# Second input projection of a two-layer kernel: six column blocks by one level of Strassen's algorithm, in two passes of half the tokens

## The chip, the cores and the metric

One Trainium2 chip, one core. The metric is the device time of one execution in microseconds (us). The kernel runs as a single launch.

## The reference

Two blocks over a sequence of 2048 tokens with width 1024, in float32. The first is RMS norm, a pooling mixer and a residual. The second takes its output, normalises and modulates it, and does

```python
proj = h @ w_in + b_in                      # (2048, 1024) @ (1024, 4624)
na_q, na_k, na_v, na_z, ml_q, ml_k, ml_v, ml_o, ml_z, i_f, f_f, i_b, f_b = split(proj)   # nine blocks of 512, four gates of 4
na_out = neighbourhood_attention(na_q, na_k, na_v, rpb) * silu(na_z)
qk = silu(centred_short_conv(concatenate([ml_q, ml_k]), conv_w, conv_b))                 # 5 taps over the tokens
hm = (mlstm forward + mlstm backward) * sigmoid(ml_o)
ml_out = normalised(hm) * ml_norm_w * silu(ml_z)
y = concatenate([na_out, ml_out]) @ w_out
```

with a gated residual and a final RMS norm. The change is in `h @ w_in` and in what stands directly around it.

## The kernel before, in words

Each engine runs one instruction stream in order; semaphores tie them together, and the order within each stream is written out by hand. SyncE (SP) and GpSimd (POOL) issue the DMAs, a few come from ScalarE (ACT).

**Precision.** Every large operand is held as two float32r parts, high (a ScalarE copy) and low (a VectorE subtraction). `mm3` (lines 143 to 147) multiplies high x high, high x low and low x high: three matmuls for each 128x128 by 128x512 piece.

**Stages.** `Mixer` and `FirstOut` make the first block, whose output goes to DRAM transposed as hT2. While `FirstOut` runs, `GatedWeights` multiplies `w_out` by the gate, splits it and stores it. `Proj` is the second input projection, `States` the mLSTM gates and states, `Attention` the neighbourhood attention, `Tail` the rest.

**Proj before.** All of h stays in SBUF as split halves (`iT`, 4 token blocks of 512). Nine blocks of 512 weight columns follow one another: nq, nk, mv, mk, mq, nv, nz, mz, mo. Six are column blocks: a unit is 128 weight columns, stationary, with 512 tokens moving, one item (24 matmuls) for each unit and token block. mv, nv and mo are row blocks: an item is 128 tokens, stationary, by 512 columns, again 24 matmuls. Each weight unit is loaded once (512 KB, line 1389) and split once (lines 1438 and 1443). After an item its PSUM bank is read: ScalarE adds the bias or takes SiLU (lines 1544, 1562, 1567), VectorE makes the low part of nq and nk (line 1633), the five taps of the convolution for mk and mq (line 1618) or the bias sum of the row blocks (line 1653), ScalarE takes the sigmoid of mo (line 1578), and GpSimd issues the stores (mk and mq at line 1672, mo at line 1697).

**States.** `States` is called after each item on every engine, one tick an item, from the fourth nv item on (first the gates, then 31 steps). A step loads keys (lines 2312, 2318) and values into the one buffer `sv` (line 2322, on SyncE, after the previous step's weighing), weighs them on GpSimd into the one buffer `swv` (line 2378), multiplies (line 2397), updates the state on VectorE (line 2358) and stores it (line 2327). TensorE's step at an item uses the weighing that GpSimd did one tick earlier.

**The end of Proj before.** 16 mo items. At mo item 3 SyncE issues attention's first 16 loads of 256 KB (`hd`, line 1835), at 7 its z and v loads, at 11 its tables (line 1852). Attention's first scores stand before the last mo item's matmuls (`first_pe`).

## Time and profile before

| | |
|---|---|
| Time, median of 3 runs | 1884.34 us (1883.26 to 1884.55) |
| Profiled execution: span | 1883.3 us |
| Profiled execution: own time | taken as its span, no other figure is shown |
| TensorE busy | 1865.6 us, 99% |
| VectorE, ScalarE, GpSimd busy | 982.4, 618.3, 552.5 us (52, 33, 29%) |
| Granted TensorE clock, mean | 0.999 of 2.4 GHz |
| DMA | 303.55 MB, mean 161 GB/s |

Rows of matmuls give the duration of one from its start to its end; they overlap, so their distance is shorter. Waits that a row attributes to a releaser are inferred from semaphore events. Windows give, for each stretch, its length and each engine's busy time with the number of instructions, the granted clock as a share of 2.4 GHz, the DMA engines' busy share and GB/s.

### The profile page before, as it was taken

Reading aid. Unit: us, or ns where it says so; the run is one execution under the profiler, and the core shown is the slowest. Engines: PE = TensorE matmul, PEld = TensorE weight load, DVE = VectorE, ACT = ScalarE, POOL = GpSimd, SP = SyncE. Lnnn points to the kernel's source line nnn. Section 1 sums busy time; section 2 is a strip of 40 time slices with the busy share of each in tenths; the row PEclk is TensorE's granted clock in tenths of the full one; section 3 lists DMA queues with packets and bytes.
Section 4 is the critical chain, followed back from the end, with each engine's and each line's share of the span. In section 5 each row is a group of like instructions: output and inputs, shape, how many; then the busy total and the mean of one; then the engine's idle time right before and its main releaser. Section 6 shows DMA issues by size and latency. Waiting matters only on the chain.

```text
span 1883.3 us, 26698 instructions
## 1 busy us (share of the span) xinstructions
PE 1865.6 (99%) x10035; PEld 1540.4 (82%) x10035; DVE 982.4 (52%) x2117; ACT 618.3 (33%) x1317; POOL 552.5 (29%) x925
## 2 busy tenths in 40 slices
PE   9999999999999999999999999999999999999998
PEld 8888878888888888888888787888887777788886
DVE  6556565775666433114777322223213777776665
ACT  7321111233444432101222202221114667655552
POOL 2112222233642222110110000222314777544442
PEclk9999999999999999999999999999999999999999
DMA  6223142366897745312221123665563776867663
GB/s 197 95 79 119 62 128 81 104 184 235 306 266 252 235 168 162 101 50 84 74 78 68 53 62 116 211 211 171 168 220 105 243 232 224 271 219 241 230 229 112
DMA packets 236365, 303.55 MB, mean 161 GB/s; under 512 B 41414, under 2 KB 161126, under 8 KB 236204
## 3 DMA queue, kind: packets, MB, share of 16 engines
q1 hardware_dynamic: 205724, 215.84, 37.4%
q0 software_dynamic: 23600, 77.61, 11.4%
q10 hardware_dynamic: 6912, 8.39, 1.2%
q8 instruction: 80, 1.31, 0.3%
q14 instruction: 49, 0.40, 0.1%
HBM read 194.71 MB, written 107.54 MB: 160 GB/s over the span
## 4 chain that ended last, share of the span: by engine, by line
PE 94%; DVE 2%; DMA 2%; issue 1%; ACT 1%; POOL 0%; SPq 0%; POOLq 0%; DVEq 0%; ACTq 0%
PE banks L145 25%; PE banks L147 25%; PE banks L146 25%; PE banks L2106 3%; PE banks L2069 3%; PE banks L2088 3%; PE banks L2704 2%; PE banks L2706 1%; PE banks L2397 1%; DMA iraw<-in_w_in 1%; PE banks L2089 1%; PE banks L2674 1%; PE banks L234 1%; PE banks L1109 1%; PE banks L1741 0%
## 5 line engine op out<-in xcount | busy, mean ns | idle before, releaser
L145 PE MATMUL banks<-hT,wu 128*128 128x512 f32 (+1 forms) x528 | 204.6, 387 | 1.1 <-DVE wu L512 0.6
L147 PE MATMUL banks<-hT,wu 128*128 128x512 f32 (+1 forms) x528 | 202.3, 383 | 0.0
L146 PE MATMUL banks<-hT,wu 128*128 128x512 f32 (+1 forms) x528 | 202.2, 383 | 0.0
L145 PE MATMUL banks<-iT,wub 128*128 128x512 f32 x384 | 151.2, 394 | 0.0
L145 PE MATMUL banks<-iT,wua 128*128 128x512 f32 x384 | 150.8, 393 | 0.0
L145 PE MATMUL banks<-wub,iT 128*128 128x512 f32 x384 | 150.6, 392 | 0.0
L147 PE MATMUL banks<-iT,wub 128*128 128x512 f32 x384 | 149.7, 390 | 0.0
L147 PE MATMUL banks<-iT,wua 128*128 128x512 f32 x384 | 149.5, 389 | 0.0
L146 PE MATMUL banks<-wub,iT 128*128 128x512 f32 x384 | 149.5, 389 | 0.0
L147 PE MATMUL banks<-wub,iT 128*128 128x512 f32 x384 | 149.5, 389 | 0.0
L146 PE MATMUL banks<-iT,wua 128*128 128x512 f32 x384 | 149.5, 389 | 0.0
L146 PE MATMUL banks<-iT,wub 128*128 128x512 f32 x384 | 149.4, 389 | 0.0
L1653 DVE TENSOR_TENSOR st<-banks,br 128x512 f32<-128x512 f32 x48 | 33.1, 692 | 201.0 <-PE banks L147 193.5
L145 PEld LDWEIGHTS banks<-hT,wu 128*128 128x128 f32 x528 | 99.3, 188 | 25.3 <-ACT ub L470 4.3
L147 PEld LDWEIGHTS banks<-hT,wu 128*128 128x128 f32 x528 | 99.2, 188 | 19.6
L146 PEld LDWEIGHTS banks<-hT,wu 128*128 128x128 f32 x528 | 99.3, 188 | 18.5
L1932 ACT ACTIVATE p<-s,ast 128x480 f32<-128x480 f32 (+1 forms) x128 | 83.7, 655 | 53.0 <-DVE ast L1970 53.0
L145 PE MATMUL banks<-ws,ys 128*128 128x512 f32 x256 | 100.5, 393 | 0.0
L147 PE MATMUL banks<-ws,ys 128*128 128x512 f32 x256 | 99.8, 390 | 0.0
L146 PE MATMUL banks<-ws,ys 128*128 128x512 f32 x256 | 99.7, 389 | 0.0
L1618 DVE SCALAR_TENSOR_TENSOR ca<-cu,cw,ca 128x512 f32<-128x512 f32 (+2 forms) x128 | 96.3, 752 | 4.5
L2039 POOL TENSOR_SCALAR p<-p,ast 128x384 f32<-128x384 f32 (+1 forms) x128 | 71.9, 562 | 46.2 <-DVE ast L1976 44.8
(293 smaller groups left out, 4116.3 us busy)
## 6 DMA issues: line engine op xcount, KB each, us to landing
iraw<-in_w_in SPq DMA_DIRECT2D x36, 512.0 KB, 4.4
wa<-in_w_ada SPq DMA_DIRECT2D x48, 256.0 KB
...
xr<-in_x SPq DMA_DIRECT2D x16, 512.0 KB, 4.4
h<-h POOLq DMA_DIRECT2D x16, 512.0 KB, 4.3
hT<-tr POOLq DMA_DIRECT2D x16, 512.0 KB, 5.1
tws<-wg SPq DMA_DIRECT2D x16, 512.0 KB, 5.1
```

The lines of the kernel that those rows point to most:

```text
L145: e.matmul(ps, lh, rh, start=first, stop=False)
L146: e.matmul(ps, lh, rl, start=False, stop=False)
L147: return e.matmul(ps, ll, rh, start=False, stop=last)
L234: t = e.transpose(self.tp[m][g][:, j * P:(j + 1) * P], self.x[m][:, (4 * g + j) * P:(4 * g + j + 1) * P], self.ident[:])
L1618: e.scalar_tensor_tensor(out=a[:, left:right], in0=cur[:, left + x:right + x], scalar=cw[:, x, ch:ch + 1], in1=a[:, left:right], op0=ALU.m ...
L1653: e.tensor_tensor(self.st[i % 2][:], pb, self.br[:, x % 2, :], ALU.add).then_inc(*self.row_step.inc())
L1932: e.activation(self.pr[n % 8][:, 0:N], self.sr[n % 4][:, 0:N], ACT.Exp, bias=self.st[:, n, 0:1], scale=-1.0, accum_out=self.st[:, n, 1:2]) ...
L2039: e.tensor_scalar(rows[:, :, 0:P], rows[:, :, 0:P], self.st[:, n, 2:3], 1.0, ALU.mult, ALU.mult).then_inc(*self.scaled.inc())
L2069: t = e.matmul(self.pS[(2 * p + hh) % 4][:, 0:N], b[r, q, (2 * i + a) * P:(2 * i + a + 1) * P], keys, start=x == 0, stop=x == 2)
L2088: e.transpose(self.pT[x][:, j * P:(j + 1) * P], probs[:, 160 * j:160 * j + P], self.ident[:])
L2106: t = e.matmul(self.pO[d, 0:P], v, self.ptr[(2 * q + hh) % 4][r, j * P:(j + 1) * P], start=(j == 0), stop=(j == nb))
L2704: t = e.matmul(o, self.eb[c % 2][d][:, h, :], self.v1[c % 2][:, h, :], start=True, stop=not self.inter(c, d))
```

## The change

The six column blocks are grouped in pairs of units (a quad: two units of 128 columns by two token blocks of 512, the 1024 of the sum cut in two). A quad takes seven products of 12 matmuls instead of eight (Strassen's algorithm in Winograd's form). The tokens are done in two passes of 1024: in each, mv, gates, nv (and in the first pass mo) as row items for 8 token tiles, then 12 quads, and after the second pass's quads the last 8 mo items.

Per quad, GpSimd forms four sums of weights (S1 to S4) before they are split; per pass it forms four sums of tokens (T1 to T4), 1024 wide, in two rounds. Seven weight operands a quad are split on ScalarE and VectorE, 512 wide, into a ring of nine slots. Products 1, 6, 7, 4 follow one another in one PSUM bank and 5, 3 in another without a new start, so the sums of products arise in PSUM; ScalarE copies the partial sums out after 5, 1 and 6, and TensorE goes on in that bank when the copy is made. VectorE joins copy, bank and bias (`join`), and for a convolution quad does four taps on each of two token blocks (the first tap is now ScalarE's); GpSimd stores.

States' ticks lie beside the second pass's quads (every second or third product) and then two to an item in the first seven mo items, on TensorE one in the middle and one at the end of an item. The state has two buffers now; `sv` and `swv` still one each. Attention's first 16 loads are issued at mo item 0, the tables at 1, z and v at 4. ml_norm_w is multiplied into the gated weights and no longer into mz.

The diff, cut to its core:

```diff
-def mm3(e, ps, lh, ll, rh, rl, first, last):
-
-    e.matmul(ps, lh, rh, start=first, stop=False)
-    e.matmul(ps, lh, rl, start=False, stop=False)
-    return e.matmul(ps, ll, rh, start=False, stop=last)
+def mm3(e, ps, lh, ll, rh, rl, first, last, more=False):
+    e.matmul(ps, lh, rh, start=first, stop=False, skip_group_check=more)
+    e.matmul(ps, lh, rl, start=False, stop=False, skip_group_check=more)
+    return e.matmul(ps, ll, rh, start=False, stop=last, skip_group_check=more)
...
+            if j // 2 < 4:
+                e.tensor_tensor(self.lo[j % 2][:], self.raw[j % 2][:], self.hi[j % 2][:].bitcast(F32), ALU.subtract).then_inc(*self.low.inc())
+            else:
+                w.wait_ge(*proj.col_in.ge(5))
+                e.scalar_tensor_tensor(out=self.lo[j % 2][:], in0=self.raw[j % 2][:], scalar=proj.mw[:, j // 2 - 4:j // 2 - 3],
+                                       in1=self.hi[j % 2][:].bitcast(F32), op0=ALU.mult, op1=ALU.subtract).then_inc(*self.low.inc())
...
+QUADS = ((("mk", "nz"),) * 4 + (("mq", "mz"),) * 4 + (("nk", "nq"),) * 4,
+         (("mk", "nz"),) * 4 + (("nk", "nq"),) * 4 + (("mq", "mz"),) * 4)
+COLUMN = {"nq": 0, "nk": 1, "nv": 2, "nz": 3, "mq": 4, "mk": 5, "mv": 6, "mo": 7, "mz": 8}
 ROW_BLOCKS = ("mv", "nv", "mo")
+NQ = 12
+PRODUCTS = 7 * NQ
...
+        work = [("mv", m) for m in range(8)] + [("gates", 0), ("gates", 1)] + [("nv", m) for m in range(8)] + [("mo", m) for m in range(8)]
...
+        work += self.products(0)
...
+        work += [("mv", m) for m in range(8, NT)] + [("gates", 2), ("gates", 3)] + [("nv", m) for m in range(8, NT)]
...
+        work += self.products(1)
+        self.mo0 = len(work)
+        work += [("mo", m) for m in range(8, NT)]
+        self.work = work
...
+                q = x[2]
+                self.place.append({"5": self.y[q % 2], "3": self.y[q % 2], "2": self.z}.get(x[0], self.x[q % 2]))
...
+        out = [("5", ps, 0)]
+        for q in range(NQ):
+            out += [(x, ps, q) for x in "12637"] + ([("5", ps, q + 1)] if q < NQ - 1 else []) + [("4", ps, q)]
+        return out
...
+        at = {11: [("t", 0, 0)], 13: [("t", 0, 1)], self.second + 9: [("t", 1, 0)], self.second + 11: [("t", 1, 1)]}
+        for ps in range(2):
+            c0 = self.c0[ps]
+            for q in range(NQ):
+                for steps, n in ((("S1", "S3"), 7 * q - 9), (("S2",), 7 * q - 6), (("S4",), 7 * q - 4)):
+                    if q == 0 and steps[0] == "S1":
+                        n = -2
+                    at.setdefault(c0 + max(n, -2 if q == 0 and steps[0] == "S1" else -1), []).extend(("s", ps, q, x) for x in steps)
+            at[c0 - 1].sort(key=lambda x: (x[2], ("S2", "S4", "S1", "S3").index(x[3])))
...
+        c0 = self.c0[1]
+        at = [c0 + 2 * i for i in range(18)] + [c0 + 36 + 2 * i for i in range(11)] + [c0 + 59 + 3 * i for i in range(9)]
+        self.ticks = {n: [i] for i, n in enumerate(at)}
+        t = len(at)
+        for m in range(7):
+            self.ticks[self.mo0 + m] = [t + 2 * m, t + 2 * m + 1]
+        self.ticks_sp = {}
+        order = sorted(self.ticks)
+        for a, b in zip(order, order[1:]):
+            self.ticks_sp.setdefault(a + 1 if a + 1 < b else b, []).extend(self.ticks[b])
...
+        if j[0] == "a":
+            w.wait_ge(*self.full.ge(self.product_of(j) + 1))
+        elif j[2] == 7:
+            w.wait_ge(*self.full.ge(self.last_item(j[1]) + 1))
+        else:
+            w.wait_ge(*self.kdone.ge(7 * j[1] + j[2] + 1))
...
+        s = (q + 1) % 2
+        r = self.raw[s].rearrange("p a (k c) -> p (a k) c", k=4)
+        if q < 2:
+            w.wait_ge(*self.done(("row", 2 + 2 * ps, 3 + 4 * q)))
+        else:
+            w.wait_ge(*self.done(("a", ps, q - 2, ("S4", "S3", "A22")[part])))
+        name, j = self.unit(ps, q, part > 0)
+        c = COLUMN[name] * W + j * P
+        ks = (slice(0, KT), slice(0, 4), slice(4, KT))[part]
+        dst = (slice(0, KT), slice(KT, KT + 4), slice(KT + 4, 2 * KT))[part]
+        e.dma_start(r[:, dst], self.win[:, ks, c:c + P]).then_inc(*self.raw_in[s].inc())
...
     def sp(self, e, att, states):
...
+            if n >= mo0:
+                att.early_sp(e, w, n - mo0)
+            for t in self.ticks_sp.get(n, ()):
+                states.sp(e, w, t)
...
+    def act_task(self, e, w, ps, q, t):
+        g, cu, ca, key = self.g, self.cu, self.ca, (ps, q)
+        conv = self.kind(ps, q) == "conv"
+        if t in (1, 3):
+            x, b = ("1", 0) if t == 1 else ("6", 1)
+            w.wait_ge(*self.full.ge(self.item[(x, ps, q)] + 1))
+            self.copy_wait(w, ps, q, x)
+            if not conv:
+                self.free(w, ("g0", "g1")[b], (ps, q, b))
+            else:
+                for y in [y for y in self.nkq if y < (ps, q)][-1:]:
+                    self.stored(w, y + (b,))
+                if (ps, q) == (0, 0):
+                    for i in range(2):
+                        w.wait_ge(*self.out.t_st[i].ge(8))
+            e.activation(g[b][:], self.bank(ps, q, x), ACT.Copy).then_inc(*self.copied.inc())
+        if conv:
+            i = self.convs[key]
+            ch = (4 if QUADS[ps][q][0] == "mk" else 0) + q % 4
...
+                w.wait_ge(*self.joined.ge(3 * NQ * ps + 3 * q + 1 + x))
+                w.wait_ge(*self.conv_u.ge(3 * i + (1, 3)[x]))
+                self.free(w, ("ca0", "ca1")[x], (ps, q, x))
+                e.activation(ca[x][:, left:right], cu[x][:, left:right], ACT.Identity, bias=self.cb[:, ch:ch + 1],
+                             scale=self.cw[:, 0, ch:ch + 1]).then_inc(*self.tapped.inc())
+            if t == 6:
+                w.wait_ge(*self.joined.ge(3 * NQ * ps + 3 * q + 3))
+                e.activation(g[5][:], g[5][:], ACT.Silu).then_inc(*self.evac.inc())
...
+            if t in (6, 9):
+                x = t // 9
+                left, right = self.edge(ps, x)
+                w.wait_ge(*self.conv_step.ge(8 * i + 4 * x + 4))
+                e.activation(ca[x][:, left:right], ca[x][:, left:right], ACT.Silu).then_inc(*self.evac.inc())
+        else:
+            if t in (3, 5):
+                x = t // 5
+                w.wait_ge(*self.joined.ge(3 * NQ * ps + 3 * q + 1 + x))
...
+            if name == "5":
                 w.wait_ge(*self.full.ge(n + 1))
+                self.copy_wait(w, x[1], x[2], "5")
+                e.activation(self.g[2][:], self.pg(n), ACT.Copy).then_inc(*self.copied.inc())
+            for ps, q, t in self.tasks(n):
+                self.act_task(e, w, ps, q, t)
...
+    def join(self, e, w, ps, q, t):
+        g, cu = self.g, self.cu
+        conv = self.kind(ps, q) == "conv"
+        c = 3 * NQ * ps + 3 * q
+        if t not in (2, 4, 5):
+            return
+        x = {2: "2", 4: "3", 5: "7"}[t]
+        w.wait_ge(*self.full.ge(self.item[(x, ps, q)] + 1))
+        w.wait_ge(*self.copied.ge(c + {2: 2, 4: 3, 5: 1}[t]))
+        pb, b = self.bank(ps, q, x), self.bias(ps, q, int(t == 5))
...
+    def dve_task(self, e, w, ps, q, t):
+        g, cu, ca = self.g, self.cu, self.ca
+        c = 3 * NQ * ps + 3 * q
+        if self.kind(ps, q) == "conv":
+            i = self.convs[(ps, q)]
+            ch = (4 if QUADS[ps][q][0] == "mk" else 0) + q % 4
+            x = int(t > 5)
+            left, right = self.edge(ps, x)
+            for y in {3: (1, 2), 4: (3,), 5: (4,), 6: (1, 2), 7: (3,), 8: (4,)}.get(t, ()):
+                w.wait_ge(*self.tapped.ge(2 * i + x + 1))
+                if y > 1:
+                    w.wait_ge(*self.conv_step.last())
+                e.scalar_tensor_tensor(out=ca[x][:, left:right], in0=cu[x][:, left + y:right + y], scalar=self.cw[:, y, ch:ch + 1],
+                                       in1=ca[x][:, left:right], op0=ALU.mult, op1=ALU.add).then_inc(*self.conv_step.inc())
+            return
+        if t in (4, 6):
...
+            for ps, q, t in self.tasks(n):
+                self.join(e, w, ps, q, t)
+            for j in due:
+                self.split_low(e, w, j)
+            for ps, q, t in self.tasks(n):
+                self.dve_task(e, w, ps, q, t)
...
+        r = lambda y: self.a_raw(ps, q, y)
+        w.wait_ge(*self.raw_in[(q + 1) % 2].ge(self.raw_loads(("a", ps, q))))
+        if x == "S1":
+            if q:
+                w.wait_ge(*self.done(("a", ps, q - 1, "S2")))
+                w.wait_ge(*self.sums.last())
+            elif ps == 0:
+                for i in range(2):
+                    w.wait_ge(*self.out.t_st[i].ge(8))
+            e.tensor_tensor(r("S1"), r("A21"), r("A22"), ALU.add).then_inc(*self.sums.inc())
+        elif x == "S3":
+            w.wait_ge(*self.sums.last())
+            e.tensor_tensor(r("S3"), r("A11"), r("A21"), ALU.subtract).then_inc(*self.sums.inc())
+        elif x == "S2":
+            w.wait_ge(*self.done(("a", ps, q, "S1")))
+            e.tensor_tensor(r("S2"), r("S1"), r("A11"), ALU.subtract).then_inc(*self.sums.inc())
+        else:
+            w.wait_ge(*self.done(("a", ps, q, "A12")))
+            w.wait_ge(*self.sums.last())
+            e.tensor_tensor(r("S4"), r("A12"), r("S2"), ALU.subtract).then_inc(*self.sums.inc())
+    def stores(self, e, w, ps, q, t):
+        k, key = self.k, (ps, q)
...
+            for s in self.sums_at.get(n, ()):
+                self.sum(e, w, s)
+            for ps, q, t in self.tasks(n):
+                self.stores(e, w, ps, q, t)
...
+                    e.dma_start(k.s[name][x[1] * P:(x[1] + 1) * P, :], st[:]).then_inc(*self.lane[lane].inc())
...
             out.tail_pool(e, w, n)
+            for t in self.ticks.get(n, ()):
+                states.pool(e, w, t)
...
+                    if y == 3 and n >= self.mo0:
+                        for tick in self.ticks.get(n, ())[0:1]:
+                            states.pe(e, w, tick)
...
+                c = 3 * NQ * ps + 3 * q
+                if name in "637":
+                    w.wait_ge(*self.copied.ge(c + {"6": 2, "3": 1, "7": 3}[name]))
+                elif name == "4":
+                    w.wait_ge(*self.joined.ge(c + 3))
+                a = ("a", ps, q, {"5": "S1", "1": "A11", "2": "A12", "6": "S2", "3": "S4", "7": "S3", "4": "A22"}[name])
+                w.wait_ge(*self.done(a))
+                s = self.slot(a).rearrange("p s (k c) -> p s k c", k=4)
+                o, ready = self.moving(ps, name)
+                for y in range(4):
+                    w.wait_ge(*self.done(ready[y // 2]))
+                    t = mm3(e, pb, s[:, 0, y, :], s[:, 1, y, :], o[:, 0, y], o[:, 1, y], y == 0 and name in "512", y == 3,
+                            name in "6374")
+                t.then_inc(*self.full.inc())
             out.tail_pe(e, w, n)
+            for tick in self.ticks.get(n, ())[int(row):]:
+                states.pe(e, w, tick)
...
+    def early_sp(self, e, w, i):
         proj = self.proj
+        if i == 0:
+            w.wait_ge(*proj.full.ge(proj.mo0))
             for name in ("nq", "nk"):
                 proj.stored_all(w, name)
             for j in self.jobs:
                 if j[0] == "q":
                     self.load(e, w, 0, j)
+        if i == 1:
+            for j in self.jobs:
+                if j[0] == "t":
+                    self.load(e, w, 0, j)
+        if i == 4:
             proj.stored_all(w, "nz")
...
     def first_pool(self, e, w):
+        w.wait_ge(*self.proj.full.ge(len(self.proj.work)))
         self.scale(e, w, 0)
...
...
             c, d, i = self.at(s)
             dcB = self.k.gates_out[4]
+            state, old = self.state[i % 2], self.state[(i + 1) % 2]
+            if i >= 2:
+                w.wait_ge(*self.cd_st[i % 2].ge(i // 2))
             for h in range(4):
                 w.wait_ge(*self.product.ge(2 * i + h // 2 + 1))
                 src = self.pU[h // 2][:, (h % 2) * (P + 1):(h % 2 + 1) * (P + 1)]
                 if s in (0, NT):
+                    e.tensor_copy(state[:, h, :], src).then_inc(*self.updated.inc())
                 else:
                     w.wait_ge(*self.updated.ge(4 * i))
+                    e.scalar_tensor_tensor(out=state[:, h, :], in0=old[:, h, :], scalar=dcB[:, 4 * d + h, c:c + 1], in1=src,
```

`tasks` calls, at item t of a quad, what belongs to step t (0 to 10); steps 7 to 10 fall beside the next quad's first items. `free` and `stored` wait until a buffer's last store has landed.

## Rows read from the trace of the kernel before

**Rows 1.** The page, parts 1 and 4: busy time of engines, the chain that ended last.
```profile
PE 1865.6 (99%) x10035; PEld 1540.4 (82%) x10035; DVE 982.4 (52%) x2117; ACT 618.3 (33%) x1317; POOL 552.5 (29%) x925
...
PE 94%; DVE 2%; DMA 2%; issue 1%; ACT 1%; POOL 0%; SPq 0%; POOLq 0%; DVEq 0%; ACTq 0%
```

**Rows 2.** Windows: the states beside nz and mz (first), the convolution blocks (second).
```profile
1186.00:1277.00 91.00, 91.00 (x480) 77.84 (x479) 23.32 (x58) 20.08 (x30) 22.68 (x27) 1.00 0.68 213
...
869.00:1048.00 179.00, 179.00 (x791) 144.61 (x790) 127.69 (x210) 49.30 (x76) 17.55 (x32) 1.00 0.23 77
```

**Rows 3.** Waits of TensorE, longest in total first: total us, times, longest.
```profile
PE banks L2240 <- DVE dg L2213: 1.8, 1, 1.8
```

**Rows 4.** The page, part 5: one of nine such groups of projection matmuls.
```profile
L145 PE MATMUL banks<-iT,wub 128*128 128x512 f32 x384 | 151.2, 394 | 0.0
```

**Rows 5.** Timeline of VectorE, mo items: start us, us, instruction, [idle before <-releaser].
```profile
1424.66 0.69 DVE L1653 TENSOR_TENSOR st<-banks,br 128x512 f32<-128x512 f32 x1 [4.75 <-PE banks L147]
1430.10 0.69 DVE L1653 TENSOR_TENSOR st<-banks,br 128x512 f32<-128x512 f32 x1 [4.75 <-PE banks L147]
```

**Rows 6.** One line or tile each: duration ns min/median/max, first and last start.
```profile
L1618 DVE SCALAR_TENSOR_TENSOR ca<-cu,cw,ca x128: 749/752/757, 876.1 to 1044.7; 128x512 f32<-128x512 f32 x64, 128x510 f32<-128x510 f32 x32, 128x514 f32<-128x514 f32 x32
...
L1188 DVE TENSOR_TENSOR glo<-graw,ghi x16: 681/684/686, 453.2 to 540.1; 128x512 fp32r<-128x512 f32 x16
...
L1544 ACT ACTIVATE cu<-banks,bc x32: 668/672/674, 874.1 to 1041.1; 128x512 f32<-128x512 f32 x32
...
L2647 POOL TENSOR_TENSOR eb<-nb,mask x32: 1270/1294/1764, 1590.8 to 1836.2; 128x512 f32<-128x512 f32 x32
...
L2358 DVE SCALAR_TENSOR_TENSOR state<-state,dcB,banks x112: 335/344/353, 1193.4 to 1395.4; 128x129 f32<-128x129 f32 x112
...
L2378 POOL TENSOR_TENSOR swv<-sv,wT x30: 1046/1067/1071, 1179.5 to 1376.1; 128x516 f32<-128x516 f32 x30
```

**Rows 7.** The stores of mk at line 1672, issue and landing.
```profile
L1672 POOL DMA_DIRECT2D mk<-ca x16: 542/542/742, 880.2 to 960.0; - x16
...
DMA to landing us min/median/max: 2.5/3.1/4.0
```

**Rows 8.** Timeline of VectorE in the last stage.
```profile
1642.22 1.28 DVE L2684 SCALAR_TENSOR_TENSOR eb<-banks,eb 128x512 f32<-128x512 f32 x2
1643.41 2.87 DVE L2691 TENSOR_TENSOR ib<-ib,q 128x512 f32<-128x512 f32 x2
```

**Rows 9.** Timeline of GpSimd, same stretch.
```profile
1642.74 2.99 POOL L2647 TENSOR_TENSOR eb<-nb,mask 128x512 f32<-128x512 f32 x2
```

**Rows 10.** The chain that ended last in order of time: one state step's matmuls.
```profile
1291.34 0.89 PE banks L2397 x8
```

**Rows 11.** Timeline of SyncE: first and last of attention's 16 early loads.
```profile
1373.88 0.32 SPq L1835 DMA_DIRECT2D hd<-nqh  x1
...
1384.16 0.82 SPq L1835 DMA_DIRECT2D hd<-nkl  x1
```

**Rows 12.** The tile sv: its loads, issue to landing.
```profile
DMA to landing us min/median/max: 3.0/3.4/4.8
```

**Rows 13.** Line 1835, the loads of hd: issue ns, landing us.
```profile
L1835 SPq DMA_DIRECT2D hd<-nql x16: 319/432/1066, 1374.2 to 1552.4; - x16
...
DMA to landing us min/median/max: 3.9/6.1/9.7
```

**Rows 14.** Timelines of ScalarE and GpSimd after one mo item (that of 1424.66).
```profile
1425.39 0.63 ACT L1578 ACTIVATE st<-st 128x512 f32<-128x512 f32 x1 [4.81 <-DVE st L1653]
...
1426.31 0.54 POOL L1697 DMA_DIRECT2D mo<-st  x1 [4.90 <-ACT st L1578]
```

**Rows 15.** Windows at the end of the program; the clock is third from last.
```profile
1876.00:1878.00 2.00, 0.00 (x0) 0.00 (x0) 0.15 (x1) 1.15 (x2) 0.56 (x1) 1.00 0.00 0
1878.00:1880.00 2.00, 0.00 (x0) 0.00 (x0) 1.28 (x1) 0.00 (x0) 0.00 (x0) 0.51 0.00 0
```

**Rows 16.** The page, part 6: loads of the projection's weights before.
```profile
iraw<-in_w_in SPq DMA_DIRECT2D x36, 512.0 KB, 4.4
```

1144 lines of the change are left out of this document (686 added, 458 removed).

## The prediction

> **What bounds the kernel now.** I read the page first. TensorE is busy for 99% of the span and the chain that ended last is 94% TensorE [rows 1]. So an edit that takes matmuls out of the projection can pay in full, and one that makes TensorE wait costs in full. The stage windows come next: over the second projection TensorE is busy for the whole of every window at a granted clock of 1.00, while VectorE stands at 71% where the convolution blocks run, and ScalarE and GpSimd lower [rows 2]. The reader should see that the other engines have room now, but not much on VectorE in exactly the part that the change loads further. The waits confirm it: TensorE's longest wait in the whole program is 1.8 us [rows 3]. Gain and loss will therefore be: matmuls taken out, minus new waits of TensorE.
>
> **What comes out.** Projection matmuls are 9 groups of 384, that is 3456, with 128x512 outputs [rows 4]. Two thirds, 2304, belong to the six column blocks (24 units x 4 token blocks x 24). The change does them in 2 passes x 12 quads x 7 products x 12 matmuls = 2016 of the same shape, so 288 go. The price of one: two evacuations of consecutive row items start 5.44 us apart, an item has 24 matmuls, so 0.227 us [rows 5]. (The 0.39 us of a matmul row is its latency, the matmuls overlap.) 288 x 0.227 = 65.3 us. The row blocks, the gates and the states' matmuls keep their count. This term is nearly certain unless the products' matmuls run slower, for which no row speaks: in before the same shapes go at the same pace with either operand stationary.
>
> **What is added on the other engines, and what hides it.** Per convolution quad TensorE works 7 products x 12 x 0.227 = 19.0 us. In that time:
> ScalarE gets 3 copies, 2 taps, 4 SiLU and 7 splits, 16 operations of 0.6 to 0.7 us [rows 6], about 10 us: covered.
> VectorE gets 7 low splits at 0.684, 8 taps at 0.752, 3 joins at 0.69 and 3 edge copies of four columns, for which I take 0.17, half of the 0.34 of a 128-column operation: 4.8 + 6.0 + 2.1 + 0.5 = 13.4 us [rows 5, 6]: covered on its own.
> GpSimd gets 4 operand sums at 1.29 and 4 stores of 0.54 [rows 6, 7], about 7 us: covered on its own.
> But these two are not independent. Two VectorE operations on SBUF operands took 2.87 us together beside GpSimd's tensor-by-tensor products, where two operations of the same size with one operand in PSUM took 1.28 just before [rows 8, 9]. So a GpSimd sum can hold VectorE up for most of its own 1.3 us. With four sums, VectorE's need is up to 13.4 + 5.2 = 18.6 us of 19.0. The Trainium skill, page "SBUF — State Buffer", section "Who interferes with whom", says that a VectorE instruction with two SBUF inputs and a GpSimd instruction that reads SBUF exclude each other for a whole instruction; by that rule all splits and taps are exposed, and it speaks against this change. The trace agrees (2.87 us).
> In the second pass the states and their gates ride along. A state step brings 4 VectorE operations at 0.344 (1.4 us) and a GpSimd product of 1.07 [rows 6], against 0.89 us more of TensorE [rows 10]. The last four quads of that pass carry 2.33 steps each: VectorE 18.6 + 2.33 x 2.45 = 24.3, TensorE 19.0 + 2.1 = 21.1, so up to 3.2 us a quad, 13 in all. The four quads with the gates: about 2 us more VectorE each, up to 1.5 us a quad, 6 in all. The nk/nq quads have no taps (about 10.6 us of VectorE) but 3.5 steps: within 1 us of even, 2 in all. The eight convolution quads of the first pass: up to 0.5 us each, 4. Full collision thus gives 25 us; no collision gives nothing but isolated waits like those of before, some 3 us. A store that lands late (3.1 us, up to 4.0 [rows 7]) holds the tap on ScalarE, and behind it the copy that the next matmul chain waits for; by my count that copy is still about 1 us early, which is thin, so the upper end is 35. I take 13, about half of the full collision, because VectorE's own waits absorb part.
>
> **The last part: eight mo items with the states' end inside.** Before, state steps came one per item of 5.44 us, 16 mo items stood at the end, and attention's first loads were issued only when the states' loads were out. Now the ticks 38 to 49 (12 state products) sit two to an item in the first six mo items, and SyncE, at mo item 0, issues attention's 16 loads first and only then the load of v for step 20. Without waits: 8 x 5.44 + 12 x 0.89 = 54.2 us, already in the base. Waits, counted from T0, the end of the products:
> First wait. The 16 loads took SyncE 1373.88 to 1384.98, 11.1 us [rows 11]. Then 0.3 for the kT load, v lands 3.4 us after its issue in calm traffic and 6.1 behind such loads [rows 12, 13], GpSimd weighs it in 1.07: T0 + 15.9 to 18.6; I take 17.5. TensorE wants it at the end of item 0, T0 + 2.7 + 0.9 + 2.7 = 6.3. Wait 11.2 us. With faster issue (0.43 each [rows 13]) and 3.0 us landing it is 5, with the 9.7 us landing it is 16.
> End of each item. The tick at an item's end needs wv from the GpSimd tick that stands behind the mo store of the same item. That store waits for the VectorE sum and the ScalarE sigmoid: sum starts at 1424.66, store is issued by 1426.85, so 2.2 us after the item's end, plus 1.07, a wait of 3.3 us [rows 5, 6, 14]. In before, the weighed tile was a full item old when TensorE used it. Items 1 to 5: 16.5 us.
> Middle of each item. v is one buffer: its next load waits for the weighing. Landing 3.4 + 1.07 = 4.5 us after the last weighing, while TensorE arrives 0.89 + 2.72 = 3.6 after it: 0.9 us, five times, 4.5 us.
> Sum 11.2 + 16.5 + 4.5 = 32 us, minus 1 for roundings and overlap: 31. From 20 (short first wait, table and z loads cost nothing) to 42. Queued behind TensorE's wait are the item's second half and the next items; nothing later has slack to give it back, since attention's first scores follow at once. GpSimd's wait added before attention's first scaling costs nothing: in before that scaling already started after the last mo item.
> A wait of 11 us also concerns the clock. After the program's last matmul the clock still stood at 1.00 (2.4 GHz) for one window of 2 us without matmuls, and at 0.51, the 1.2 GHz level, in the next [rows 15]. So the long wait will very likely drop the clock, and some matmuls after it run at the lower level. The row gives no price for coming back; I hold 1 to 4 us for it in the range. The Trainium skill, page "TensorE: Matmul & The Clock Gate", section "HAM oscillation — how this bites in real kernels", also warns of idle gaps in mid-kernel; the fall in the rows agrees.
>
> **Costed at nothing.** Row blocks re-split per pass (48 slots instead of 12 units): one item is 5.4 us, eight splits at 0.684 are 5.5, and one slot is free ahead; TensorE reads the slots in order, so no wait. If DMA were late, some us at each of five boundaries. Each weight block is loaded twice, 36 x 512 KB or 18 MB more [rows 16]; it meets a DMA share of 0.23 to 0.68 [rows 2]. The ml_norm factor moved into the gated weights: same instruction count. GpSimd's two rounds of eight 1024-wide sums run beside nv items, which store from SyncE.
>
> **The sum.** The profiled execution's own time is its span, 1883.3 us; the median of the three runs is 1884.3, 1.0 above. 1884.3 - 65.3 = 1819.0; + 13 (products) + 31 (mo part) = 1863.
>
> **Rivals.**
> A. Forecast: gain half eaten, by the mo part more than by the products. 1840 to 1880. For it: the order of instructions on SyncE and GpSimd, which is fixed. Chance 0.60.
> B. Gain mostly kept: attention's loads issue at 0.43 us and the end-of-item wait is shorter than I read: mo 12, products 3: 1834; range 1822 to 1840. Against it: the store stands before the weighing in GpSimd's program. Chance 0.14.
> C. VectorE and GpSimd become the bound of the products (the rule on SBUF above): convolution quads run at the pace of VectorE plus blocked time plus the ring of store, tap, split, tap. With 3 us over TensorE's 19.0 in each of 16 convolution quads, 48, and the mo part 31: 1898. It decides from (65.3 - 31) / 16 = 2.1 us a quad. For it: 18.6 of 19.0 before any delay. Against it: collisions need both at work, and GpSimd waits much. Chance 0.16, with 0.12 of it above 1888.
> D. Losses just balance: 1880 to 1888. 0.10.
>
> Below 0.2% (about 4 us) a run of this kernel cannot be told from no change. Faster 0.76, same 0.11, slower 0.13. Range 1836 to 1892; A's own is 1845 to 1880.
>
> **What would show it.** Projection matmuls 3168 instead of 3456, still 0.227 apart inside a product. In the mo part: a TensorE wait of about 11 us at the end of mo item 0 with SyncE issuing hd loads, then waits of about 3 us on the weighed tile at each item's end. A clock digit below 9 there. VectorE 75 to 95% busy in convolution quads, with splits and taps longer than 0.75 us beside GpSimd sums. Wrong, if TensorE waits in the products come to more than 35 us, or if the mo part runs without gaps.

## The result and the profile after

The changed kernel took 1904.2 us (median of four, 1898.9 to 1912.6) where the kernel before took 1884.1 beside it: ratio 1.0105, interval 1.0078 to 1.0132. The forecast of 1863 was 41 us too low, and the result lies above the range. Span of the profiled execution: 1901.2 us, against 1883.3 - 65.3 = 1818.0 with the removed matmuls alone: 83 us are missing.

The page, parts 1 and 4, answering to [rows 1], with the clock's digits of part 2 between them:

```profile
PE 1830.1 (96%) x9747; PEld 1500.1 (79%) x9747; DVE 1165.1 (61%) x2348; ACT 756.8 (40%) x1552; POOL 741.6 (39%) x1037
...
PEclk9999999999999999999999999999778999999999
...
PE 88%; DMA 3%; DVE 3%; POOL 2%; issue 1%; SPq 1%; ACT 1%; POOLq 0%; DVEq 0%; ACTq 0%
```

288 matmuls are gone (10035 to 9747), but TensorE is idle for 71 us instead of 18, and three slices show a lower clock. The waits of TensorE in total, answering to [rows 3]:

```profile
PE banks L2882 <- POOL swv L2863: 37.2, 6, 18.4
PE banks L2894 <- DMA skC<-mk: 10.9, 4, 3.7
PE banks L158 <- DVE ring L1592: 1.8, 1, 1.8
PE banks L158 <- DVE pg L1938: 1.6, 1, 1.6
```

Both large waits are in state steps: for the weighed tile (mo part) and for the key tile (second pass of products). The windows, in the order nv and mo items, nk/nq quads of the second pass, mo part:

```profile
700.00:750.00 50.00, 50.00 (x220) 40.80 (x219) 19.24 (x22) 13.41 (x20) 12.53 (x13) 1.00 0.28 86
...
1200.00:1250.00 50.00, 42.76 (x211) 35.83 (x210) 25.38 (x55) 17.27 (x33) 24.30 (x29) 0.93 0.79 249
...
1348.00:1454.00 106.00, 68.83 (x293) 56.31 (x293) 27.74 (x76) 11.86 (x19) 20.81 (x25) 0.76 0.58 184
```

The mo part has 69 us of work in 106, at a mean clock of 0.76. In the first window TensorE never waits, yet it does 220 matmuls in 50 us. The same window of the kernel before has 222:

```profile
700.00:750.00 50.00, 50.00 (x222) 41.39 (x221) 15.43 (x28) 14.10 (x29) 9.76 (x18) 1.00 0.51 158
```

**Inside the mo part.** Timeline of TensorE, the items' state products and a few matmuls behind them. The first two lines are item 0, before any wait:

```profile
1347.38 1.05 PE L2882 MATMUL banks<-swv,skT 128*128 128x129 f32 x8
...
1351.00 1.05 PE L2882 MATMUL banks<-swv,skC 128*128 128x129 f32 x8
...
1373.21 2.09 PE L2882 MATMUL banks<-swv,skT 128*128 128x129 f32 x8 [18.38 <-POOL swv L2863]
...
1375.95 0.63 PE L160 MATMUL banks<-late,op 128*128 128x512 f32 x1
1376.37 0.63 PE L158 MATMUL banks<-late,op 128*128 128x512 f32 x1
...
1378.64 0.39 PE L158 MATMUL banks<-late,op 128*128 128x512 f32 x1
...
1379.34 1.05 PE L2882 MATMUL banks<-swv,skC 128*128 128x129 f32 x8
...
1382.77 0.40 PE L160 MATMUL banks<-late,op 128*128 128x512 f32 x1
1386.81 2.09 PE L2882 MATMUL banks<-swv,skT 128*128 128x129 f32 x8 [3.64 <-POOL swv L2863]
```

Behind the wait of 3.64 us, as behind that of 18.38, the products take 2.09 us instead of 1.05 and matmuls start 0.42 us apart instead of 0.23: the 1.2 GHz level. The profile's granted clock says the same; in the window inside the long wait its mean is already 0.56, and the DMA engines' share is 0.97:

```profile
1356.00:1370.00 14.00, 0.00 (x0) 0.00 (x0) 4.08 (x7) 2.52 (x3) 0.56 (x1) 0.56 0.97 321
```

The half item behind a wait takes 6.13 us (1373.21 to 1379.34), the same half of item 0 took 3.62 (1347.38 to 1351.00): 2.5 us for the lower clock. The item's other half ends 3.83 us after its start (1383.17), and with the wait of 3.64 that is 13.6 us an item. The sixth and last wait (3.65 us) differs a little: its product still takes 1.16 us, and matmuls start 0.42 us apart only from 1.5 us later on, which costs 1.7 us. Why the wait, from the timelines of VectorE, ScalarE and GpSimd:

```profile
1383.21 0.69 DVE L2025 TENSOR_TENSOR pg<-banks,br 128x512 f32<-128x512 f32 x1 [7.27 <-PE banks L160]
...
1383.93 0.63 ACT L1904 ACTIVATE pg<-pg 128x512 f32<-128x512 f32 x1 [21.07 <-DVE pg L2025]
...
1385.10 0.58 POOL L2143 DMA_DIRECT2D mo<-pg  x1 [7.56 <-ACT pg L1904]
1385.70 1.06 POOL L2863 TENSOR_TENSOR swv<-sv,wT 128x516 f32<-128x516 f32 x1
```

The order is the one forecast: bias sum, sigmoid, store, weighing, then TensorE. The first wait, from SyncE's timeline, and then the tile sv in the same stretch (the weighing of it, and the landing of its loads):

```profile
1347.57 0.32 SPq L2321 DMA_DIRECT2D hd<-nqh  x1
...
1357.11 0.57 SPq L2321 DMA_DIRECT2D hd<-nkl  x1
1357.73 1.33 SPq L2803 DMA_DIRECT2D skT<-kTD  x1
1359.10 0.57 SPq L2807 DMA_DIRECT2D sv<-mv  x1
```

```profile
L2863 POOL TENSOR_TENSOR swv<-sv,wT x1: 1046/1046/1046, 1372.1 to 1372.1; 128x516 f32<-128x516 f32 x1
...
DMA to landing us min/median/max: 3.2/8.1/12.9
```

The 16 loads are issued as fast as expected (10.1 us), but the load of v behind them lands after 12.9 us; I had taken 3.4 to 6.1.

**The matmuls' own pace.** Timeline of TensorE in a mo item without any wait:

```profile
702.35 0.39 PE L159 MATMUL banks<-ring,op 128*128 128x512 f32 x1
702.58 0.39 PE L160 MATMUL banks<-ring,op 128*128 128x512 f32 x1
702.80 0.40 PE L158 MATMUL banks<-ring,op 128*128 128x512 f32 x1
...
703.26 0.40 PE L160 MATMUL banks<-ring,op 128*128 128x512 f32 x1
703.50 0.39 PE L158 MATMUL banks<-ring,op 128*128 128x512 f32 x1
703.73 0.40 PE L159 MATMUL banks<-ring,op 128*128 128x512 f32 x1
703.97 0.39 PE L160 MATMUL banks<-ring,op 128*128 128x512 f32 x1
```

From 702.80 the starts are 0.234 us apart, before that 0.227. It lasts for 12 matmuls in each item of 24: those that read the four ring slots at 188.125 to 200.125 KB. An item takes 5.53 us instead of 5.44, a quad 19.28 instead of 19.05.

### The profile page after: what moved, and what is told of

It is laid out like the page before. It is cut to its first block, busy times and chain, and to the rows that moved or that the text cites. A ratio compares the mean times of both kernels' runs of the same rounds, so it can differ in the third digit from the quotient of the medians.

```text
span 1901.2 us, 27025 instructions
## 1 busy us (share of the span) xinstructions
PE 1830.1 (96%) x9747; PEld 1500.1 (79%) x9747; DVE 1165.1 (61%) x2348; ACT 756.8 (40%) x1552; POOL 741.6 (39%) x1037
## 4 chain that ended last, share of the span: by engine, by line
PE 88%; DMA 3%; DVE 3%; POOL 2%; issue 1%; SPq 1%; ACT 1%; POOLq 0%; DVEq 0%; ACTq 0%
PE banks L158 24%; PE banks L160 24%; PE banks L159 24%; PE banks L2592 3%; PE banks L2555 2%; PE banks L2574 2%; PE banks L3189 1%; PE banks L3191 1%; PE banks L2882 1%; DMA skC<-mk 1%; DMA sv<-mv 1%; PE banks L3159 1%; PE banks L247 1%; PE banks L1122 1%; PE banks L2575 1%
## 5 line engine op out<-in xcount | busy, mean ns | idle before, releaser
L158 PE MATMUL banks<-op,ring 128*128 128x512 f32 x672 | 267.2, 398 | 3.1 <-DVE pg L1938 1.6
L160 PE MATMUL banks<-op,ring 128*128 128x512 f32 x672 | 264.2, 393 | 0.0
L159 PE MATMUL banks<-op,ring 128*128 128x512 f32 x672 | 264.1, 393 | 0.0
L158 PEld LDWEIGHTS banks<-op,ring 128*128 128x128 f32 x672 | 127.0, 189 | 31.6 <-DVE pg L1938 2.0
L160 PEld LDWEIGHTS banks<-op,ring 128*128 128x128 f32 x672 | 126.9, 189 | 28.4
L159 PEld LDWEIGHTS banks<-op,ring 128*128 128x128 f32 x672 | 127.1, 189 | 27.0
L1973 DVE SCALAR_TENSOR_TENSOR ca<-cu,cw,ca 128x512 f32<-128x512 f32 (+2 forms) x128 | 113.5, 887 | 35.8 <-ACT ca L1831 34.6
L1592 DVE TENSOR_TENSOR ring<-praw,ring 128x512 fp32r<-128x512 f32 x160 | 130.8, 841 | 5.6 <-ACT ring L1587 5.3
L158 PE MATMUL banks<-ring,op 128*128 128x512 f32 x320 | 126.5, 395 | 1.8 <-DVE ring L1592 1.8
L160 PE MATMUL banks<-ring,op 128*128 128x512 f32 x320 | 126.4, 395 | 0.0
L159 PE MATMUL banks<-ring,op 128*128 128x512 f32 x320 | 126.2, 394 | 0.0
L2025 DVE TENSOR_TENSOR pg<-banks,br 128x512 f32<-128x512 f32 x48 | 33.1, 689 | 150.7 <-PE banks L160 131.6
L1587 ACT ACTIVATE ring<-praw 128x512 fp32r<-128x512 f32 x160 | 97.0, 622 | 54.1 <-PE banks L160 48.6
L159 PEld LDWEIGHTS banks<-hT,wu 128*128 128x128 f32 x528 | 99.3, 188 | 18.4
L158 PE MATMUL banks<-ws,ys 128*128 128x512 f32 x256 | 100.5, 393 | 0.0
L160 PE MATMUL banks<-ws,ys 128*128 128x512 f32 x256 | 99.8, 390 | 0.0
## 6 DMA issues: line engine op xcount, KB each, us to landing
opraw<-hT SPq DMA_DIRECT2D x17, 1024.0 KB, 10.1
```

The lines of the kernel that those rows point to most:

```text
L158: e.matmul(ps, lh, rh, start=first, stop=False, skip_group_check=more)
L159: e.matmul(ps, lh, rl, start=False, stop=False, skip_group_check=more)
L160: return e.matmul(ps, ll, rh, start=False, stop=last, skip_group_check=more)
L1587: e.activation(h, src, ACT.Copy).then_inc(*self.hi.inc())
L1592: e.tensor_tensor(l, src, h.bitcast(F32), ALU.subtract).then_inc(*self.lo.inc())
L1973: e.scalar_tensor_tensor(out=ca[x][:, left:right], in0=cu[x][:, left + y:right + y], scalar=self.cw[:, y, ch:ch + 1], in1=ca[x][:, left:ri ...
```

## The experiments

Each ran beside the kernel before, whose median varied from 1884.1 to 1886.5 us; ratios compare best. The interval of the changed kernel's own ratio is 5 us wide to either side, so a difference to it of less than about 6 us cannot be told from none. Kernels 1 to 13 are edits of the changed kernel, 14 of the kernel before; the diffs are shortened to their core. By the ratio the changed kernel stands 20 us above the kernel before.

**1. Attention's loads spread out.**

```diff
-  if i == 0: the 16 loads of hd          # ahead of states.sp at mo item i
+  # behind states.sp: (3, 3, 3, 3, 2, 2, 0, 0)[i] loads of hd
```

> Edit: SyncE issues attention's 16 first loads (256 KB each) not ahead of the states' loads of mo item 0, but three, three, three, three, two and two of them behind the states' loads of mo items 0 to 5. Nothing else changes. Theory (the load of v for step 20 was late behind the 16 loads): TensorE's wait of 18.4 us at the end of mo item 0 falls to the 3.6 us of the later items; the waits at the ends of items 1 to 5 stay near 3.6. Time about 1904 - 15 - some clock given back = 1886 (1880 to 1890). Rival (the 4 MB have to be moved beside the states' loads anyway, so the wait only changes place): the ends of items 1 to 5 wait 5 to 6 us each and the time falls by less than 6 us, 1898 or more.

1902.4 us, ratio 1.0087 (1.0072 to 1.0102). The first wait went from 18.4 to 6.5 us, now for a state update, but the ends of later items waited 7.2, 3.6, 4.0, 9.1 and 3.6. By the time and the mean of the waits (5.5 us) the rival is right. Three loads of 256 KB between two state steps do make the next load of v late (6.0 and 6.7 us to its landing instead of 3.0), but the waits there stayed at 3.6 and 4.0. The long ones, 7.2 and 9.1, are at items 1 and 4, where the tables, and z and v, are still issued ahead of the states' loads as well (8.4 and 8.9 us to landing).

**2. Weighing before the store.**

```diff
+  if n >= mo0: states.pool(e, w, ticks[n][0])   # ahead of the mo store
```

> Edit: in the mo items GpSimd weighs for the first of the item's two state steps before it issues the mo store, instead of behind it. Nothing else changes. Theory (the weighing stood behind a store that waits for VectorE and ScalarE): the five waits of about 3.7 us at item ends vanish; what then paces an item is the chain of the single v tile, load 3.4 + weighing 1.07 = 4.5 us a step, 9.0 to 9.6 us an item against 13.65 now and 7.2 without any wait. Time about 1904 - 5 x 4.2 = 1883 (1878 to 1890). Rival (the wait at the end of an item is for the landing of v, not for the store): the item stays above 12.5 us and the time falls by less than 6 us.

1892.2 us, ratio 1.0039 (1.0028 to 1.0050): 12 us back of 20, where 21 were expected. The wait at the second mo item's end fell from 3.6 to 2.7 and three others to 1.4; the first stayed (19.0). Items 2 and 3 took 9.0 us as expected, but one wait grew from 4.2 to 7.7 us, at item 4, where attention's z and v loads stand ahead of the load of the v tile.

**3. Both.**

> Edit: both edits before this one together (attention's loads spread behind the states' loads, first weighing of an item before its store). Theory (these two places and the lower clock behind them are about 50 of the 85 us that are missing): the mo part from the end of the products takes 62 to 72 us instead of 105; time 1904 - 36 = 1868 (1862 to 1875), faster than the kernel before the change (1884). Rival (the missing time is in the products, and what is gained here comes back as waits of attention): 1885 or more.

1895.0 us, ratio 1.0047 (1.0032 to 1.0062), no better than the second alone. GpSimd's timeline shows its weighings waiting for v:

```profile
1382.51 1.04 POOL L2872 TENSOR_TENSOR swv<-sv,wT 128x516 f32<-128x516 f32 x1 [12.24 <-DMA sv<-mv]
1387.37 1.05 POOL L2872 TENSOR_TENSOR swv<-sv,wT 128x516 f32<-128x516 f32 x1 [3.29 <-DMA sv<-mv]
1394.34 1.04 POOL L2872 TENSOR_TENSOR swv<-sv,wT 128x516 f32<-128x516 f32 x1 [5.92 <-DMA sv<-mv]
```

My theory of two places, 1868 us, fell: the single v tile is a third, and attention's traffic acts through it.

**4. Weight loads behind the states' loads** in the second pass.

```diff
-  load_quad(1, c // 7 + 2, c % 7);  states.sp(t)
+  states.sp(t);  load_quad(1, c // 7 + 2, c % 7)
```

> Edit: in the second pass of products SyncE issues the loads of weights for the quad after next (512 KB and two of 256 KB) behind the states' loads of the same item instead of ahead of them. Nothing else changes. Theory (about 20 of the missing us lie in the second pass where the keys of a state step are issued late behind such a load and land after 5 to 6 us, with TensorE waiting 10.9 us for them and its clock low for a while behind each wait): the waits for the key tile fall from 10.9 to 5 us or less, the time by 6 to 12, to about 1895. Rival (the landing is slow because all 16 DMA engines are busy with stores and weights, wherever the issue stands): waits stay at 9 us or more, time within 4 us of 1904.

1902.9 us, ratio 1.0094 (1.0077 to 1.0111); the waits for keys were 10.3 us. The rival's numbers came true: the order of these loads on SyncE is not what makes keys late. That the engines are busy, its reason, is not shown by this.

**5. Filler in TensorE's waits.**

```diff
+  for x in range((76, 14, 14, 14, 14, 14, 0)[m]): e.transpose(pT, ident, ident)
   states.pe(e, w, tick)
```

> Edit: ahead of the state step at the end of mo items 0 to 5 TensorE does transposes of the identity into a PSUM bank that nobody reads (76 at item 0, 14 at each of the others, 0.22 us each by the state's products), so that it works where it waited. This is more work and changes no result. Theory (behind each wait the granted clock is 1.2 GHz for a while, and this is what makes an item 13.65 us and not 11.3): the clock stays at 1.00 in the mo part, an item takes 11.0 to 11.6 us, the time falls by 10 to 16 us, to about 1891, with more instructions. Rival (the item's length is the chain of loads, weighing and stores, the clock only goes with it): item and time unchanged within 3 us, or longer by what the fillers overrun the waits.

1902.6 us, ratio 1.0089 (1.0070 to 1.0108). A transpose took 0.12 us, not 0.22, so the fillers covered half of each wait. Behind three of the five later waits TensorE's timeline shows the clock still up:

```profile
1400.00 1.69 PE L2186 MATMUL banks<-ident 128*128 128x128 f32 x14
1403.81 1.16 PE L2891 MATMUL banks<-swv,skT 128*128 128x129 f32 x8 [2.11 <-POOL swv L2872]
```

The product takes 1.16 us and not 2.09, and two items took 12.0 us instead of 13.65, though fillers and wait together are 3.8 us, hardly more than the wait before. With the clock up, waits of 0.5 and 0.6 us for v appear in the middle of these items. So the 1.6 us saved an item and these 0.6 are the price of the clock seen apart from the wait. Behind one more wait the fillers did not keep it (the product took 1.43 us and the clock was low for 3.4 us behind it), a later item took 16.4, and the first wait still ended at the late load. The 10 to 16 us expected did not come: the whole gained nothing that can be told.

**6. Operand sums cut thin.** GpSimd's sums cover 4 of 512 columns, so the weights of most products are not the right sums.

> Edit: GpSimd's operand sums (128x512) are cut to 4 of their 512 columns, but for the first quad of the first pass, so the weights of the products are mostly not the right sums; every other instruction is unchanged. This takes away nearly all that collides with VectorE in the products. Theory (collisions lengthen VectorE's splits and taps, but TensorE hardly waits for them): taps fall from 0.89 to about 0.75 us, the period of a quad in the first pass from 19.28 to 19.05 to 19.1 us, the time by 3 to 8 us in all. Rival (VectorE and GpSimd are the bound of the products, as by my third rival on record): 25 us or more come back.

1902.7 us, ratio 1.0085 (1.0068 to 1.0101). VectorE's taps of 512 columns and splits in the first pass, by form, with full sums (first fence) and thin ones (second):

```profile
L1592 DVE TENSOR_TENSOR ring<-praw,ring 128x512 fp32r<-128x512 f32 x53 | 45.9, 881 | 2.2 <-ACT ring L1587 2.2
L1973 DVE SCALAR_TENSOR_TENSOR ca<-cu,cw,ca 128x512 f32<-128x512 f32 x32 | 32.2, 1006 | 0.3
```

```profile
L1592 DVE TENSOR_TENSOR ring<-praw,ring 128x512 fp32r<-128x512 f32 x53 | 35.5, 686 | 11.8 <-ACT ring L1587 11.8
L1973 DVE SCALAR_TENSOR_TENSOR ca<-cu,cw,ca 128x512 f32<-128x512 f32 x32 | 23.9, 747 | 0.3
```

The collisions are real, 10 and 8 us in these groups, and they vanish with the sums. But TensorE's pace stayed (219 matmuls in the 50 us from 700 on, as against 220) and its single waits of 1.8, 1.6 and 1.5 us too. So the shorter quads and the 3 to 8 us that I expected did not come either. The third rival on record is refuted, and the pace is not VectorE's doing.

**7. Attention's loads last**, weighing first.

```diff
-  hd at mo item 0, tab at 1, z and v at 4, each ahead of states.sp
+  hd, tab, z and v behind states.sp of mo item 5
```

> Edit: GpSimd weighs ahead of the mo store as in the second experiment, and SyncE issues all of attention's first loads (16 of 256 KB, the tables, z and v) behind the states' loads of mo item 5, none before. The first experiment showed that even three of them between two state steps make the load of the v tile late. Theory (the single v tile and its load behind attention's loads set the pace): mo items 0 to 5 take 9.0 to 9.8 us each, then one wait of 5 to 12 us for attention's loads at the end; mo part 105 - 30 = 75 us or less, time 1872 (1866 to 1880). Rival (the loads have to be waited for somewhere, so nothing is gained over the second experiment): 1888 or more.

1887.7 us, ratio 1.0010 (0.9999 to 1.0020). The time, 1872 expected, was missed. Four items took 9.0 to 9.2 us, as expected of one v tile, but the first took 15.4, with a wait of 5.4 us for a state update. It stands in VectorE's program behind the row sum and behind two splits of tokens, 1024 wide (VectorE's timeline):

```profile
1355.55 2.36 DVE L1592 TENSOR_TENSOR op<-opraw,op 128x1024 fp32r<-128x1024 f32 x2 [1.64 <-ACT op L1587]
```

The first wait of experiments 3, 8, 11 and 12 is for a state update too, and of 5.4 to 5.9 us. At the end TensorE stood still for 17.7 us ahead of its first score, more than I allowed. The profile names no releaser for that wait; that it is for attention's loads is my reading.

**8. State steps earlier.**

```diff
-  [c0 + 36 + 2*i for i in range(11)] + [c0 + 59 + 3*i for i in range(9)], then 2 x 7
+  [c0 + 36 + 2*i for i in range(24)], then 2, 2, 2, 2, 1, 1
```

> Edit: GpSimd weighs ahead of the mo store; state steps go on at one in two products until the end of the second pass (24 of them instead of 20), so that the mo items carry 2, 2, 2, 2, 1 and 1 instead of 2 each for seven; attention's first loads are issued behind the states' loads of mo item 3. Theory (VectorE and GpSimd have room in the last quads, two steps in an item don't fit the v tile's 4.5 us a step): four items of 9.0 to 9.8 us and four of 5.4 to 6.4, the last quads of the second pass longer by no more than the 3.6 us of the four steps; time 1862 (1855 to 1870). Rival (the last quads are full: VectorE at over 90% there makes TensorE wait): the four quads take 4 us each more, time 1878 or more.

1882.4 us, ratio 0.9987 (0.9974 to 0.9999), where 1862 was expected. Waits: 14.2 us for keys, 9.8 for the state, 7.5 ahead of attention's first scores. The mo items came out as expected but for the first (15.7, then 9.0, 9.0, 8.1, 5.5 and 5.5 us). The products did not: they ended 13 us later than in the changed kernel, where 3.6 were allowed. The time is the rival's, its reason is not: VectorE was busy for 68 to 76% there, and most of the waits are for keys.

**9. Ring slots 128 bytes further.**

```diff
-  ring: 188.125, 192.125, 196.125, 200.125, 0, 4, 8, 12, 16 (KB)
+  ring: 188.25, 192.25, 196.25, 200.25, 0, 4, 8, 12, 16
```

> Edit: four of the nine slots of the ring that holds the split weights (and the small tile behind them) are moved by 128 bytes, from 188.125 to 188.25 KB and so on; no instruction changes otherwise. The trace shows the matmuls that read these four slots 0.234 us apart and those of the other five 0.227; in the kernel before, every weight tile began at a whole number of KB and all went at 0.227. Theory (the address of the slot within a KB sets the pace of the matmul): all go at 0.227, a row item falls from 5.53 to 5.44 us, a quad from 19.28 to about 19.1, the time by 8 to 12 us, to about 1893. Rival (it is the region, or the splits that ScalarE and VectorE write to the neighbours meanwhile): no change.

1899.9 us, ratio 1.0067 (1.0053 to 1.0081). Matmuls that read the ring now start 0.227 us apart throughout; items take 5.44, quads 19.04. (The mo part reads other tiles, which were not moved; it stayed at 0.231 where the clock was up.) In the second pass the kernel is 5.5 us ahead at its first copies (one at 1080.2 instead of 1085.7); 2.5 of these are lost again by its end, beside keys that still land late. By the ratio it is 7 us, with some 6 us of uncertainty, of the nine that the pace should give; in the trace 5.5 us are plain.

**10. Two key tiles.** The kernel before holds the same key tile; the change did not touch it.

```diff
-  if s >= 1: wait turned >= s;  load k(s) into kC
+  if s >= 1: wait turned >= s;  load k(s + 1) into kB[(s + 1) % 2]
```

> Edit: the key tile of the states that TensorE transposes gets a second buffer, so SyncE issues each key load one state step earlier. Nothing else changes. Theory (the 10.9 us that TensorE waits for keys in the second pass, and the lower clock behind these waits, come from the single tile, whose load lands 5 to 6 us after it may be issued): these waits fall below 2 us, the second pass gets shorter by 10 to 20 us, time 1890 (1884 to 1896). Rival (the DMA engines are full there, at a share of 0.76, and something else is late instead: stores, weights, states): less than 5 us come back.

1888.6 us, ratio 1.0017 (1.0008 to 1.0026). The waits for keys in the second pass are gone, and so are two stretches of 3.4 us each at the lower clock that stood behind the two longest of them. The window with these reads, before and after this edit:

```profile
1196.00:1280.00 84.00, 75.73 (x372) 63.35 (x371) 49.84 (x105) 30.25 (x55) 40.35 (x46) 0.96 0.76 235
```

```profile
1196.00:1280.00 84.00, 83.38 (x430) 70.14 (x429) 59.84 (x117) 36.25 (x66) 48.77 (x53) 1.00 0.87 268
```

The DMA engines had room for it: their share rose from 0.76 to 0.87.

**11. Two v tiles as well**, weighing first, attention's loads 3, 3, 3, 3, 4 and the rest behind item 5.

```diff
-  wait weighed >= i;  load v(i) into v
+  wait weighed >= i;  load v(i + 1) into (v, vB)[(i + 1) % 2]     # from i = 16 on
```

> Edit: two key tiles and two v tiles, first weighing of a mo item before its store, attention's 16 loads 3, 3, 3, 3 and 4 behind the states' loads of mo items 0 to 4 and its other loads behind item 5; state steps where the change put them (two in each of the mo items) and the slots of the ring as they are. Theory (not the number of steps in an item but the single v tile, the store ahead of the weighing and the loads ahead of v made the mo part long): mo items at 7.3 to 8.0 us, mo part 58 to 66 us instead of 105, and the keys' 10 to 20 us: time 1848 (1840 to 1858). Rival (two steps an item are too many in themselves, the state's own chain of product, update and product limits them): items stay at 9 us or more, time 1862 or more.

1858.1 us, ratio 0.9855 (0.9841 to 0.9868), 10 us above the expectation and at the very end of its range. Three items took 9.0 us and the others 10.1 and more, as the rival had it, not 7.3 to 8.0. Waits at the six item ends were 5.4, 1.4, 1.4, 2.5, 1.4 and 5.3 us. The profile puts about half of them down to the state's update and half to the landing of the keys in the tile skT:

```profile
PE banks L2906 <- DMA skT<-kTD: 9.1, 3, 5.3
PE banks L2906 <- DVE state L2863: 8.2, 3, 5.4
```

**12. All together.**

> Edit: all together: slots moved by 128 bytes; two key tiles and two v tiles for the states, each loaded one step earlier; first weighing of a mo item before its store; a state step after every second product until the end of the pass, so 2, 2, 2, 2, 1 and 1 in the mo items; attention's 16 loads four by four behind the states' loads of mo items 0 to 3, tables behind item 4, z and v behind item 5. Theory (the missing 85 us are 10 of matmul pace, some 20 of the keys, some 50 of the v tile, the store and attention's loads in the mo part, with the clock that falls behind each wait counted in these): about 65 of them come back, time 1840 (1832 to 1850). Rival (with the waits gone, VectorE or the DMA engines are full in the last quads): 1860 or more.

1851.5 us, ratio 0.9817 (0.9804 to 0.9831), 11.5 above the expectation and below the rival's 1860. Its waits:

```profile
PE banks L2908 <- DVE state L2865: 8.7, 3, 5.9
PE banks L2908 <- DMA skT<-kTD: 3.8, 1, 3.8
```

**13. The state's update before the row sum.** VectorE's program had the update of the item's first step behind the row sum, which waits for the item's last matmul.

```diff
+  if n >= mo0: states.dve(e, w, ticks[n][0])
   w.wait_ge(*self.full.ge(n + 1))
...
```

> Edit: the twelfth kernel with everything together, and in the mo items VectorE updates the state of the item's first step before it adds the bias row of the item instead of behind it. Theory (the wait of 1.8 us at each item's end is for an update that stands behind the row sum, which itself waits for the item's last matmul): mo items with two steps fall from 8.95 to 7.2 to 7.6 us; time 1851.5 - 6 = 1846 (1842 to 1849). Rival (the chain product, update, weighing, product of the states has no room for two steps an item): items stay above 8.5 us and the time within 2 us of 1851.5.

1845.9 us, ratio 0.9782 (0.9769 to 0.9796), the fastest kernel of this study. Its waits:

```profile
PE banks L2911 <- issue: 6.5, 3, 3.7
PE banks L2911 <- POOL swv L2892: 6.3, 5, 2.2
```

The wait for the update fell from 8.7 to 0.6 us, but waits of 3.7 and less without a recorded releaser took much of its place, so items took 8.5 to 12.9 and not 7.2 to 7.6. What was gained was gained at item 0, where the update had stood behind the two splits too: the first wait fell from 5.9 to 2.2 us. The time came out right by luck, my picture of the item was wrong.

**14. The kernel before, its weight tile 128 bytes further.**

```diff
-  self.wa = k.at("wua", 188, ...)
+  self.wa = k.at("wua", 188.125, ...)
```

> Edit: in the kernel before the change the weight tile that starts at 188 KB (two of the six units) starts at 188.125 KB; nothing else changes. Theory (the address within a KB of the weight that a matmul reads sets its pace): the matmuls that read this tile go 0.233 to 0.235 us apart instead of 0.227, those of the other tile stay; a third of 3456 matmuls x 0.0067 = 7.7 us, time 1885.5 + 8 = 1893 (1890 to 1896). Rival (the pace has to do with the new ring's slots being refilled in single pieces while others are read): no change, 1884 to 1887.

1892.6 us, ratio 1.0028 (1.0017 to 1.0039). Groups of matmuls that read the moved tile and the other one, answering to [rows 4]:

```profile
L145 PE MATMUL banks<-iT,wua 128*128 128x512 f32 x382 | 151.9, 398 | 0.0
L145 PE MATMUL banks<-iT,wub 128*128 128x512 f32 x384 | 151.2, 394 | 0.0
```

Items on the moved tile take 5.57 us, those on the other 5.44. Here the moved tile is the stationary operand; in the row items of experiment 9 the ring's slots were the moving one, and both showed it. A tile's address alone made this kernel 5 us slower.

## Why the prediction was wrong

**The removed matmuls**: 288 fewer, right. "Still 0.227 apart" was wrong: four of nine slots go at 0.234. 24 quads x 0.24 + 40 row items x 0.09 = 9 us that no term held (the last 8 row items do not read the ring). I had set this aside as something "for which no row speaks"; nothing in the trace of before could show it, but the addresses in the two kernels differ, and experiment 14 shows what that does.

**The products**, 13 us forecast, for VectorE beside GpSimd. Experiment 6 prices that at nothing that TensorE feels: its waits on VectorE in the whole projection are three, 4.9 us in all, and stay without the sums. The loss was elsewhere: the key tile, 10.9 us of waits and the clock behind them. By experiment 10 the second pass gets 13.4 us shorter (between the same two copies 237.4 instead of 250.9 us). I had put DMA traffic under "costed at nothing", at a share of up to 0.68 [rows 2]; it reached 0.79, a key load took 2.8 to 6.7 us to land where it had taken 2.5 to 3.8, and a single tile has no time to spare for that.

**The mo part**, 31 us forecast, 53 found: 108.4 us from the end of the products and their state step at 1348.4 to the last item's sum at 1456.8, less 1.3 for scores, instead of 54.2.
- First wait 18.4 instead of 11.2 (range 5 to 16): the landing of v.
- Item ends: 3.64, 3.65, 3.65, 4.21 and 3.65, sum 18.8, instead of 16.5: right.
- Middle of items: none instead of 4.5. The low clock gives v the time: in experiment 5, with the clock up, 0.5 and 0.6 us of it appeared.
- Clock: 14 us (2.3 to 2.6 us behind each of five waits, 1.7 behind the sixth), where the range held 1 to 4 and the sum nothing. This is the term that was most wrong: I expected it behind the long wait alone, but it follows each of about 3.6 us. The row that I had [rows 15] showed the fall; I applied it to one wait of six. The Trainium skill, page "TensorE: Matmul & The Clock Gate", section "HAM oscillation — how this bites in real kernels", describes such a fall on every round of a loop with a short wait. The trace agrees for all six waits of this kernel. Experiment 1 has a wait of 3.64 us that was followed by a product at 1.16 us and no fall at all:

```profile
1397.15 1.16 PE L2888 MATMUL banks<-swv,skT 128*128 128x129 f32 x8 [3.64 <-POOL swv L2869]
```

Sum: 53 + 13 + 9 = 75 of 83. The three waits on VectorE make 80; the rest is not resolved.

So the steps that failed are two terms that the sum held at nothing, the clock behind the recurring waits (14 us) and the key tile under more DMA traffic (13 us), one row's pace that was carried over to tiles at other addresses (9 us), and the landing of v behind the 16 loads (18.4 us of wait for 11.2). The order of instructions, and with it the place of the waits in the mo part, was read rightly.

**The rivals.** C, VectorE and GpSimd as the bound, came nearest with its 1898 us, but by a mechanism that does not act. B fell with the mo part, D with the time. The rule on page "SBUF — State Buffer" of the Trainium skill, section "Who interferes with whom", is borne out in the durations (1.006 and 0.747 us for the same tap), but not in the time.

**The split of the mo part** between its causes is not additive: by the ratios, undoing the store's order gave 12 us, spreading the loads 3 (not told from none), both 11, and both with a second v tile and attention's other loads moved back 30 (experiment 11 against 10). That whichever of the three is left holds the chain is my reading of these four numbers; a second v tile alone was not run. What the two extra steps an item cost with perfect timing was not reached by any kernel here.
